# Plain fp32 expert products: one of 128 stationary columns, or two of 64 columns each

## The reference

```python
def grouped_moe(h, router_w, router_b, w_gate, w_up, w_down):
    ...
    # each token gets the best group of 4 experts, and the top 2 of that group
    out = jnp.zeros_like(h)
    for e in range(N_EXPERTS):                                    # 16
        a = jax.nn.silu(h @ w_gate[e]) * (h @ w_up[e])            # 1024 -> 512
        out = out + gates[..., e:e + 1] * (a @ w_down[e])         # 512 -> 1024
    return out
```

## Time and profile before

| What | Value |
|---|---|
| median of 3 runs | 677.3 us (676.62 to 677.68) |
| the profiled execution | 676.89 us, of which the traced span is 675.1 us |
| PE busy | 645.9 us (96%) |
| DVE busy | 501.4 us (74%) |
| ACT busy | 434.0 us (64%) |
| DMA in the expert stage | 0.92 to 0.93 of the 16 engines' time |

### The profile page before, as it was taken

The page is one execution under the profiler, slowest core; times in us unless marked ns, Lnnn a source line. Parts: engine busy times, 40 slices in busy tenths (PEclk is TensorE's granted clock), DMA queues, the critical chain, the costliest instruction groups (busy, mean ns, idle before and its releaser), DMA issues.

```text
span 675.1 us, 8736 instructions
## 1 busy us (share of the span) xinstructions
PE 645.9 (96%) x3026; PEld 510.5 (76%) x3026; DVE 501.4 (74%) x570; ACT 434.0 (64%) x474; POOL 18.2 (3%) x13
## 2 busy tenths in 40 slices
PE   5999999999999999999999889999999999999996
PEld 4888888778867778888877776777677767687774
DVE  4644696753775538957575779998899889989996
ACT  5543737434945446354554768789877897788781
POOL 0000000400100000000000000000000000000000
PEclk9999999999999999999999799999999999999999
DMA  9944566643632265556019437999799979998961
GB/s 338 344 154 163 214 221 232 235 165 119 214 94 94 77 233 189 187 187 187 1 46 410 204 137 301 383 383 365 298 360 388 386 280 384 382 378 308 375 243 62
DMA packets 49054, 164.04 MB, mean 243 GB/s; under 512 B 4378, under 2 KB 9180, under 8 KB 36733
## 3 DMA queue, kind: packets, MB, share of 16 engines
q1 hardware_dynamic: 44432, 158.81, 63.6%
q10 hardware_dynamic: 4588, 4.80, 2.1%
HBM read 162.53 MB, written 2.64 MB: 245 GB/s over the span
## 4 chain that ended last, share of the span: by engine, by line
PE 68%; DVE 13%; issue 8%; ACT 5%; DVEq 2%; DMA 1%; SPq 0%; POOL 0%; ACTq 0%
PE ps L1484 13%; PE ps L1476 13%; PE ps L1477 13%; PE ps L1860 8%; DVE w_lo L1232 6%; PE ps L1457 4%; PE ps L1905 3%; PE ps L1890 3%; PE ps L1842 2%; PE ps L1645 1%; DVEq L1398 1%; PE ps L1620 1%; DVE y_lo L1376 1%; DMA w_raw<-in_w_in 1%; ACT w_hi L760 1%
## 5 line engine op out<-in xcount | busy, mean ns | idle before, releaser
L901 DVE TENSOR_TENSOR w_lo<-w_raw,w_hi 128x2048 fp32r<-128x2048 f32 (+2 forms) x54 | 118.5, 2211 | 57.4 <-ACT w_hi L501 56.8
L1476 PE MATMUL ps<-w_hi,act_hi 128*128 128x512 f32 (+1 forms) x304 | 119.5, 395 | 1.5 <-ACT w_hi L501 1.5
L1477 PE MATMUL ps<-w_hi,act_lo 128*128 128x512 f32 (+1 forms) x304 | 117.0, 387 | 0.0
L501 ACT ACTIVATE w_hi<-w_raw 128x2048 fp32r<-128x2048 f32 (+2 forms) x54 | 99.1, 1855 | 26.9 <-PE ps L1484 26.1
L1232 DVE TENSOR_TENSOR w_lo<-w_raw,w_hi 128x2048 fp32r<-128x2048 f32 (+1 forms) x48 | 99.4, 2108 | 6.7 <-ACT w_hi L760 6.0
L1232 DVE TENSOR_TENSOR w_lo<-e_raw,w_hi 128x2048 fp32r<-128x2048 f32 (+2 forms) x48 | 97.3, 2064 | 1.4 <-ACT w_hi L760 1.3
L760 ACT ACTIVATE w_hi<-w_raw 128x2048 fp32r<-128x2048 f32 (+1 forms) x48 | 83.8, 1764 | 0.2 <-issue 0.2
L760 ACT ACTIVATE w_hi<-e_raw 128x2048 fp32r<-128x2048 f32 (+2 forms) x48 | 82.2, 1729 | 0.9 <-PE ps L1860 0.8
L1860 PE MATMUL ps<-w_hi,xg 128*128 128x512 f32 x236 | 75.0, 436 | 1.0 <-DVE xg L1369 1.0
L1484 PE MATMUL ps<-w_lo,act_hi 128*128 128x512 f32 (+1 forms) x304 | 74.2, 386 | 0.0
L1476 PEld LDWEIGHTS ps<-w_hi,act_hi 128*128 128x128 f32 x304 | 57.6, 190 | 14.2 <-issue 3.2
(11 more groups left out here) (317 smaller groups left out, 955.8 us busy)
## 6 DMA issues: line engine op xcount, KB each, us to landing
w_raw<-in_w_in SPq DMA_DIRECT2D x32, 1024.0 KB, 5.4
w_raw<-in_w_expert_gate SPq DMA_DIRECT2D x24, 1024.0 KB, 7.2
e_raw<-in_w_expert_down SPq DMA_DIRECT2D x24, 1024.0 KB, 7.9
w_raw<-in_w_expert_up SPq DMA_DIRECT2D x16, 1024.0 KB, 7.7
e_raw<-in_w_expert_up SPq DMA_DIRECT2D x16, 1024.0 KB, 7.8
e_raw<-in_w_expert_gate SPq DMA_DIRECT2D x8, 1024.0 KB, 9.7
w_raw<-in_w_expert_down SPq DMA_DIRECT2D x8, 1024.0 KB, 7.2
w_raw<-in_w_xkv SPq DMA_DIRECT2D x4, 1024.0 KB, 5.7
```

The costliest lines, as they stand in the source:

```text
L501: A(bview(w_hi, b, blocks[b].shape), bview(w_raw, b, blocks[b].shape), ACT.Copy).then_inc(hi_done, 1)
L901: V.tensor_tensor(bview(w_lo, b, sh), bview(w_raw, b, sh), f32(bview(w_hi, b, sh)), ALU.subtract).then_inc(lo_done, 1)
L1476: MM(o, xh[:, t0 + k, i * P:(i + 1) * P], wh[:, k], start=first and k == 0, stop=False)
L1477: MM(o, xl[:, t0 + k, i * P:(i + 1) * P], wh[:, k], start=False, stop=False)
```

## The change

Each plain product is written as two: one with the 64 hi columns into PSUM partitions 0 to 63, one with the 64 lo columns into partitions 64 to 127, in this order, with the same weights streamed by both. What is computed is the same, and the other engines' programs are untouched.

```diff
                 for t in range(nt, 4):
-                    ins = MM(ps[:, bank, :], f32(lhs[t]), raw[:, t * COLS:(t + 1) * COLS], start=False, stop=last and t == 3)
+                    for w in range(2):
+                        rows_ = slice(w * SLOTS, (w + 1) * SLOTS)
+                        ins = MM(ps[rows_, bank, :], f32(lhs[t][:, rows_]), raw[:, t * COLS:(t + 1) * COLS], start=False,
+                                 stop=last and t == 3)
                 ins.then_inc(mm_done, 1)
...
                         if c >= nt:
-                            ins = MM(ps[:, 2 + c % 2, :], f32(a_st[:, 2 * part + c // 2, :]), raw[:, c * COLS:(c + 1) * COLS],
-                                     start=False, stop=False)
+                            for w in range(2):
+                                rows_ = slice(w * SLOTS, (w + 1) * SLOTS)
+                                ins = MM(ps[rows_, 2 + c % 2, :], f32(a_st[:, 2 * part + c // 2, rows_]),
+                                         raw[:, c * COLS:(c + 1) * COLS], start=False, stop=False)
```

## The result

The changed kernel takes 683.88 us (median of 3, 683.09 to 684.55) where the kernel before takes 677.3: 1.0098 times as long, 95% interval 1.0075 to 1.0121. Slower, as forecast and clear of the noise, but by 6.6 us and not by 22.

A forecast was written before the change was run, and what follows sets the result against it. The prediction took TensorE to bound the expert stage: 13.8 us of stagger plus 10.9 of borders, less 2.5 hidden, gave +22.1 us on 677.3, so 699.4 us, range 682 to 719.

The forecast's parts named there:

- What bounds the stage: Expert stage: TensorE sets its time, busy 63.2 of 65 us, with DVE and transfers close behind.
- A pass of 64 columns costs what a wide one costs: Plain products: one record of 512 streamed columns takes 0.44 us narrow, as the wide one's 0.43.
- The stagger: Blocks with plain tiles: lo 1 starts only with hi 2, +0.43 us a block, 13.8 us over 32 blocks.
- side by side throughout: Rival: hi and lo halves of each pair run at once, only mode changes cost, 685.7 us; chance 0.20.
- The border: Going narrow and back in each plain-tile block: 0.34 us (bounds 0 and 0.68), 10.9 us over 32 blocks.
- What hides some of it: PE's wait for split weights at d2 absorbs 0.85 us in each of three groups, 2.5 us in all.
- Transfers: Expert stage weight transfers: later issue by SP delays nothing, as longer blocks leave room; counted as nothing.
- The range: Whole kernel time: 682 to 719 us, leaving no more than 2 in 10 out.

The follow-up runs named there:

- hi_only: Changed kernel with the lo product of each pair left out; 683.49 us, 1.0112 times the kernel before.
- same_half: Changed kernel with both 64-column products of a pair writing PSUM partitions 0 to 63; 714.82 us, 1.0567 times the kernel before.
- halves_apart: Changed kernel with d1 reordered: both hi products first, then both lo products; 687.07 us in one run.
- two_borders: Changed kernel with each pair's hi product behind the block's w_hi products and lo product behind its w_lo products; 722.03 us, 1.0678 times the kernel before.
- late_blocks: Kernel before with only d2 and u3 written as pairs, the other 24 blocks staying 128 columns wide; 679.55 us, 1.0042 times the kernel before.
- pair_d1: Kernel before with d1's two plain tiles each one 64-column product of unsplit activations, each in its own half; 676.86 us, 0.9992 times the kernel before.
- four_down: Kernel before with first blocks of d0, d1, d2 as four unsplit tiles in side-by-side pairs, gate and up blocks fully split; 670.27 us, ratio 0.9907.

## Why the prediction was right or wrong

- **What bounds the stage**: right. PE sets the end; the changed kernel's chain is 84% PE over the whole span, and PE alone, block after block, in the rows of the last group above.
- **A pass of 64 columns costs what a wide one costs**: right. In hi_only two passes more add 1.86 - 1.00 = 0.86, and in same_half four more add 3.58 - 1.86 = 1.72.
- **The stagger, +0.43 a block, 13.8 us**: wrong, and it is the step that made the forecast wrong. I had lo 1 wait until hi 2 had started, because it stands behind it in the program. The lo pass starts within 10 ns of the hi pass, and in halves_apart even past a whole other product. Within a run of narrow products each half works off its own in order, and lo doesn't wait for hi, in both orders that were run. The pair's stagger is thus 0 where I had 0.43. The rival "side by side throughout" (685.7 us, held at 0.20) is what happens. The Trainium skill, "TensorEngine Tiling (Array Packing)", Key Properties, has tiles operating independently, and the runs agree. The Trainium skill's sentence in "TensorE: Matmul & The Clock Gate", Part 3, that matmuls start in program order doesn't hold between halves here (halves_apart); the measurement decides. I weighed it above the first with no row for either.
- **The border, 0.34 us**: right, 0.15 in and 0.19 out, at 512 streamed columns as at 128, once a block (one pair or two), twice in two_borders. The lower bound of 0 and the upper of 0.68 were both wide of it. The Trainium skill's rule in "TensorEngine Tiling (Array Packing)", Key Properties, that a change of mode drains the engine, has this price here.
- **What hides some of it, 2.5 us**: mis-sized. 24 blocks of three groups owe 8.2 us and show 4.7, of which half a microsecond lies ahead of the first expert product, where nothing was changed: 4.0 are hidden. (A slip in the sum makes little of it: 512.93 - 512.05 is 0.88 and not 0.85, 2.6 us in three groups.) In the second group, from the start of d2 to the start of u3, the kernel before and then the changed one:

```profile
511.35 0.94 PE L1905 MATMUL ps<-w_hi,a_st 128*128 128x512 f32 x3
...
513.73 1.02 PE L1909 MATMUL ps<-w_raw,a_st 128*128 128x512 f32 x2
...
516.62 0.87 PE L1860 MATMUL ps<-w_hi,xg 128*128 128x512 f32 x3
```

```profile
515.31 0.86 PE L1908 MATMUL ps<-w_hi,a_st 128*128 128x512 f32 x3
516.00 0.86 PE L1908 MATMUL ps<-w_lo,a_st 128*128 128x512 f32 x3
...
519.78 0.86 PE L1860 MATMUL ps<-w_hi,xg 128*128 128x512 f32 x3
```

5.27 us before, 4.47 after. With its border d2 should have grown by 0.34 and shrank by 0.80: 1.14 is hidden there, 0.89 of it the wait that I had counted (from the first `w_hi` product to the first `w_lo` one 512.93 - 511.35 = 1.58 us, then 0.69). The rest, 0.25, I had not. In the kernel before, the three products behind the wait take 513.73 - 512.93 = 0.80 us instead of 0.70, 0.10 for starting again, and this goes with the wait. And the `w_lo` of the second block of d2 was late as well:

```profile
515.12 0.30 PEld L1905 LDWEIGHTS ps<-w_lo,a_st 128*128 128x128 f32 x2 [0.35 <-DVE w_lo L1232]
```

and eight products there add 2.03 us in the chain instead of 1.87. The same at d0: from its first `w_lo` product to the start of u1 it was 484.65 - 480.95 = 3.70 us, and is 486.92 - 483.05 = 3.87 now, so 0.17 of its 0.34 is hidden though its big wait stays. 1.14 + 0.17 = 1.3 us a group, 3.9 in three. The late second block by itself, 2.03 - 1.87 = 0.16, is what late_blocks showed hidden with the big wait still in place. 677.3 + 10.9 - 3.9 = 684.3, against 683.9.
- **Transfers**: right. PE's waits of the changed kernel name none. SP waits for the slots of plain blocks 77.7 us at line 1865 where it was 72.5, as PE frees them later, and 51.2 at line 1914 as before; nothing shows that a transfer came late by it.
- **The range** held the time only because it took in the rival, whose 685.7 us are 1.8 over the measured time, most of it the hidden part above. The forecast itself, +22.1 us against +6.6, was more than three times too large a step.

## What to carry to other kernels

A plain fp32 product of 64 columns costs here as much as one of 128, so cutting a wide product in two gains nothing even where the halves run side by side, and each trip to the narrow form and back costs 0.34 us. The half that a narrow product leaves free is worth filling with another tile: two plain fp32 tiles for 1.01 us, and 0.19 behind them, instead of 1.72, as soon as one operand of 64 columns holds all that is needed (here the activations before they are split). But look who is waited for first, and check the engine that a wait names against its own instructions: pair_d1 made PE's work shorter and gained nothing that its ten runs can show, since DVE set the pace there, and only edits that also took splitting off DVE brought something, up to 1.7%.

## What the runs showed of the hardware

- Plain fp32 products of 64 columns into PSUM partitions 0 to 63 and 64 to 127 overlap at no cost that the trace shows: 0.86 us for four passes of 512 streamed columns (1.01 with the border in), with the same stream and one bank (the changed kernel), with two streams and two banks (pair_d1, 1.01), and with two streams and one bank (four_down, where eight passes take 477.66 to 479.52, 1.86 with the border in).
- They pair up past each other: four narrow products ordered lower, lower, upper, upper take 1.87 us as in alternating order.
- Narrow products don't meet across a 128-column product that stands between them: in two_borders each costs its 0.86 us alone, and each change 0.15 us in and 0.19 to 0.20 out.
- When the four passes of a pair are next in line, their four weight loads are done within 0.20 us, two operands for each half; with one half alone (same_half) the third load comes 0.49 us after the first.
